# The ScalarE table that holds exponential and logarithm, loaded once in front of the differential attention of a two-block transformer kernel

## What is computed

```python
def diff_attention(q, k, v, lam, rel_bias):        # 4 heads of 2 x 64
    logits = einsum('bqhcd,bkhcd->bhcqk', qb, k) * scale + bias
    logits = where(mask, logits, -inf)
    p = softmax(logits)
    attn = p[:, :, 0] - lam * p[:, :, 1]
    return einsum('bhqk,bkhd->bqhd', attn, v)

def stick_breaking_attention(q, k, v):             # 8 heads of 64
    z = einsum('bqhd,bkhd->bhqk', qb, k) * scale
    log_1mb = where(mask, log_sigmoid(-z), 0.0)
    rem = cumsum(log_1mb, reverse=True) - log_1mb
    a = where(mask, exp(log_sigmoid(z) + rem), 0.0)
    return einsum('bhqk,bkhd->bqhd', a, v)
```

## Time and profile before

| | us |
|---|---|
| median of three runs | 2185.65 |
| lowest, highest of them | 2185.64, 2187.31 |
| the profiled execution, its own time | 2184.85 |
| its span in the trace (first to last instruction) | 2182.8 |

### The profile page before, as it was taken

One profiled execution on the slowest core, in us unless ns is written; L12 is line 12 of the kernel. 1 busy time (PEld: TensorE's weight loads), 2 busy tenths in 40 slices (PEclk: granted clock), 3 DMA queues, 4 the chain that ended last, 5 costly groups with the idle time before them and its releaser, 6 DMA issues.

```text
span 2182.8 us, 41798 instructions
## 1 busy us (share of the span) xinstructions
PE 2061.7 (94%) x17356; PEld 1271.0 (58%) x17356; DVE 863.7 (40%) x1472; ACT 477.2 (22%) x752; POOL 360.0 (16%) x389
## 2 busy tenths in 40 slices
PE   6999898599999999999999999979998998999998
PEld 5888766136434544443343333337775777888887
DVE  4454434433333323333332332333655443444444
ACT  4251433000000000000000000024445723122221
POOL 1010000112232222222232222231201200000000
PEclk9999998799999999999999999979998999999999
DMA  6333113899999999999999999963111021233231
GB/s 236 113 122 128 58 39 138 343 347 404 409 407 402 411 405 405 401 410 402 401 407 400 404 406 397 401 224 107 58 58 39 1 75 61 77 103 109 77 109 45
DMA packets 157311, 520.47 MB, mean 238 GB/s; under 512 B 16412, under 2 KB 71760, under 8 KB 124400
## 3 DMA queue, kind: packets, MB, share of 16 engines
q1 hardware_dynamic: 136480, 494.96, 57.9%
q0 software_dynamic: 20784, 24.85, 4.8%
HBM read 509.61 MB, written 18.88 MB: 242 GB/s over the span
## 4 chain that ended last, share of the span: by engine, by line
PE 63%; DMA 6%; SPq 5%; DVE 3%; ACT 2%; issue 1%; POOL 1%; ACTq 0%; DVEq 0%; POOLq 0%
PE ps L1973 24%; PE ps L1987 11%; PE ps L392 8%; PE ps L394 8%; PE ps L393 8%; DMA ring_a<-in_w_gate_up 4%; DMA ring_a<-in_w_down 2%; SPq L569 2%; SPq L567 2%; PE ps L1882 1%; POOL rstd L466 1%; PE ps L494 1%; PE ps L1874 1%; PE ps L1892 1%; PE ps L1835 0%
## 5 line engine op out<-in xcount | busy, mean ns | idle before, releaser
L1973 PE MATMUL ps<-ring_a,xe 128*32 128x512 f32 x3912 | 438.9, 598 | 12.0 <-DVE xe L1584 10.3
L1987 PE MATMUL ps<-ring_a,act_t 128*32 128x256 f32 x6000 | 335.2, 379 | 4.9 <-DMA ring_a<-in_w_down 3.0
L1973 PEld LDWEIGHTS ps<-ring_a,xe 128*32 128x32 f32 x3912 | 129.5, 111 | 294.1 <-issue 253.0
L1987 PEld LDWEIGHTS ps<-ring_a,act_t 128*32 128x32 f32 x6000 | 209.9, 110 | 137.4 <-issue 22.7
L1973 PE MATMUL ps<-ring_b,xe 128*32 128x512 f32 x2232 | 253.2, 594 | 0.0
L392 PE MATMUL ps<-xt_hi,hi 128*128 128x512 f32 x576 | 228.3, 396 | 5.6 <-DVE xt_lo L507 4.7
L394 PE MATMUL ps<-xt_hi,lo 128*128 128x512 f32 x576 | 226.3, 393 | 0.0
L393 PE MATMUL ps<-xt_lo,hi 128*128 128x512 f32 x576 | 225.8, 392 | 0.0
L1075 ACT ACTIVATE glu<-glu 128x768 f32<-128x768 f32 x32 | 27.0, 845 | 659.7 <-DVE glu L1591 618.4
L759 POOL DMA_INDIRECT x_rows<-ye,idx x96 | 154.3, 1608 | 37.8 <-issue 37.8
L1973 PEld LDWEIGHTS ps<-ring_b,xe 128*32 128x32 f32 x2232 | 76.9, 110 | 142.7 <-issue 132.6
(11 more groups left out here) (299 smaller groups left out, 2443.0 us busy)
## 6 DMA issues: line engine op xcount, KB each, us to landing
ring_a<-in_w_gate_up SPq DMA_DIRECT2D x163, 1024.0 KB
ring_a<-in_w_down SPq DMA_DIRECT2D x125, 1024.0 KB
ring_b<-in_w_gate_up SPq DMA_DIRECT2D x93, 1024.0 KB
raw<-in_w_in SPq DMA_DIRECT2D x20, 1024.0 KB, 7.7
raw<-in_w_gate SPq DMA_DIRECT2D x11, 1024.0 KB, 5.4
raw<-in_w_up SPq DMA_DIRECT2D x11, 1024.0 KB, 5.4
raw<-in_w_down SPq DMA_DIRECT2D x11, 1024.0 KB, 4.9
raw<-in_w_out SPq DMA_DIRECT2D x8, 1024.0 KB, 5.1
```

The costliest lines, as they stand in the source:

```text
L1973: last = pe.matmul(ps[QUAD * j:QUAD * j + QUAD, g, :], xe[:, g, QUAD * k:QUAD * k + QUAD], w[:, j, :, :, :], start=k == 0, stop=k == KT - 1)
L1987: last = pe.matmul(y_block(g, j), act_t[:, g, QUAD * (2 * c + h):QUAD * (2 * c + h) + QUAD], w[:, h, QF * j:QF * j + QF], start=c == 0 and ...
```

## The change

One line stands in `scalar_program` ahead of the first exponential of the differential attention. It loads the table that the compiler calls `natural_log_exp_and_others`, which holds both functions.

```diff
--- before.py
+++ after.py
@@ -980,6 +980,7 @@
                     i = copy(skT(2 * (c - B_SK) + n), bank)
                 i.then_inc(SB.evacuated[g % 4], 1)
 
+            act.preload_act_table_set("natural_log_exp_and_others")
             diff_exp(0)
             for n in range(DH * T):
                 diff_evac(n)
```

## The result

The changed kernel took 2172.53 us, the median of four runs from 2170.76 to 2174.62, beside 2186.22 for the kernel before in the same comparison. The ratio is 0.9941, with a 95% interval of 0.9926 to 0.9956: 13.7 us less where I had forecast 8.4. The time lies 1.0 us under the lower end of the range. The prediction was wrong in size, right in sign and, as the runs show, in its path.

The account below looks back on a forecast made before the run. A chain of waits with four table loads was taken to bound the kernel up to head 3's logits, then PE. 5.5 + 0.7 + 2.2 = 8.4 us off 2184.85, plus 0.80 for the median: 2177.3 us, range 2173.5 to 2181.5.

Parts of the forecast that it names:

- the second slow stretch: TensorE at 1.2 GHz in logits 3 and cumulation 2; costs 3.9 us, of which 2.2 was taken as gain.
- My own estimate of both at about 1682: Logits of head 3: without loads ready at about 1681.9, with PE free near 1682.0, within half a microsecond.
- slow stretches elsewhere: Slow clock stretches behind the stick-breaking stage: 1.7 us allowed either way, taken as 0.
- Loads on the chain: Four table loads ahead of the logits of head 3, worth 5.1 to 5.6 us together; 5.5 taken.
- Head 7: Two loads before head 7: removal shortens PE's 1.35 us wait at cumulation 7; 0.7 us taken.
- The ten hidden loads: Ten of the 16 removed loads, covered by waits for DVE or PE or by PE's work; credited with nothing.
- The added load: Load ahead of the differential attention's first exponential, inside ACT's 1.57 us idle time; cost 0, at most 1.3 us.
- The first slow stretch: TensorE at 1.2 GHz after its first wait, 1664.7 to 1671.4; worth nothing, as DVE's scaling sets head 2.
- Rival 1: TensorE falls to 1.2 GHz again near logits 3: only 6.2 us gained, median 2179.4; chance 0.31.
- Rival 2: The four chain loads were hidden by other waits: gain between none and 2 us, 2185.6 to 2183.6; chance 0.07.
- Rival 3: A table switch flushes ACT, so four chain loads give up to 10.4 us, not 5.5; 2173.2; chance 0.04.
- Rival 4: The joint table lengthens exponentials in both attentions: 2195.3 us at 0.4 us each; chance 0.03.

Follow-up runs that it names:

- e7: Changed kernel plus seven unread matmuls in TensorE's first wait, ahead of cumulation 0; 2176.81 us.
- e12: Changed kernel with two of the chain's four loads put back, before the logarithms of heads 0 and 1; 2179.40 us.
- e6: Kernel before, all 16 loads kept, with DVE's eight scaling instructions spread over heads 1 to 4; 2176.18 us.
- e5: Kernel before, all 16 loads kept, with seven unread matmuls in TensorE's wait ahead of the logits of head 3; 2180.56 us.
- e10: Changed kernel with two loads put back, before the logarithm of head 7 and the weights of head 6; 2176.68 us, a single run.
- e1: Changed kernel measured again with no edit; 2172.48 us.
- e3: Changed kernel with the ten loads put back whose removal was credited with nothing; 2175.62 us.
- e11: Changed kernel with the same ten covered loads put back, measured once more; 2172.68 us.
- e4: Changed kernel with its one load moved from the differential attention to the front of the stick-breaking attention; 2172.67 us.
- e2: Changed kernel with four loads put back, before the logarithms of heads 0, 1 and 2 and the weights of head 1; 2181.90 us.

## Why the prediction was wrong in size

**The step that failed is the clock's.** The prediction priced the second slow stretch at 3.9 us and then took 2.2, "a little over half". The trace has 3.88. The reason is not that the clock puts up with waits, as my nearest row had suggested: the wait before logits 3 vanished wholly, since PE's own work ended just as ACT was ready (e7 and e12 show that the clock would not have put up with 1.84 us). My own estimate of both at about 1682 said so, and I did not use it. That row, 1.35 us at head 7 with the clock unharmed, was one execution: e6 went unharmed too, but e5 and e10 fell at the very same wait.

**The second is the zero for slow stretches elsewhere**, with a base that was high. The profiled execution after had 2.53 us less ahead of the stage and 1.43 less behind it. Those come and go from run to run: in the differential attention a wait of 2.63 us, the same in all fourteen traces, was followed by a slow stretch in twelve, and not in the first of the changed kernel nor in e7. The stage begins at 1656.43 in e1, the same kernel as the changed one, and at 1654.43 and 1655.19 in e5 and e6, whose code is that of the kernel before up to there; from L494 to the end it takes 432.71 us in e1, and 431.68 and 431.30 in e5 and e6. Over 48 later runs before, and six of the changed kernel, the difference is 11.4 us and not 13.7. With 3.9 for the clock my sum would be 10.1. Of the 4.8 us by which the forecast of 2177.3 missed, the high base is thus 1.8 and the clock 1.7. What makes up the last 1.3 us I have not shown; it is within what single comparisons scatter (e3 and e11, one kernel, are 2.9 apart).

**The other terms held.** Loads on the chain: 5.5 taken, 5.64 measured, 1.41 for each of four, so that the overlap of two activations, 0.11 us, does belong to the price. Head 7: 0.72 taken from rows, 0.72 measured. The ten hidden loads: nothing in the stage of e3 and e11. The added load: nothing, with 0.27 us to spare as worked out. The first slow stretch: worth nothing in the first trace, as e7 shows, but where it reached into cumulation 1 (e1, e4, e10) the stage was 1.0 us longer, which the zero didn't foresee.

**The rivals.** Rival 1, the clock gives nothing back, is out: it did in both traces of the changed kernel. With 2.7 us more ladder (e12) it would have been right, and in e7 the clock fell again at a wait of 1.85 us. Rival 2, hidden anyway, is out by e2. Rival 3, a switch that costs about twice its row, gave the time nearest to what was first measured, 2173.2, by luck: a load put back moved the chain by 1.42 us (e2: 30.35 - 24.66 = 5.69 for four) and by 1.35 (e12: 2.69 for two). "ScalarE: Activation LUTs" in the Trainium skill adds a drain of about 1.38 us in its section on what ACT_TABLE_LOAD costs; these traces don't agree with it. Rival 4, slower exponentials, is out: 461 ns before and after in the stick-breaking attention, and 715 ns before and after for the exponentials of 512 columns in the differential one (L949).

## What to carry to other kernels

A short operation on ACT is worth its time only where the chain of waits passes through it, and there it can be worth nearly twice its time if the wait it lengthens leaves TensorE idle long enough to drop to 1.2 GHz (9.4 us for 5.1 us of loads in e2). So when a wait of PE is removed, count the slow groups behind it in full if PE's own work closes the gap, and nothing if a wait near 2 us or longer is left: in the stick-breaking attention each of the waits from 1.84 us up had a slow group behind it, and so had the 2.63 us of the differential one in twelve traces of fourteen. For a shorter wait give both outcomes and not the middle: behind the 1.34 to 1.35 us ahead of cumulation 7 it went either way. And where one ladder of waits has a load, a scaling and a sum in it, each of them is a handle: moving the scaling (e6, 7.7 us) was worth nearly as much as removing four loads (e2, 9.4 us).

## What the runs showed of the hardware

The same work, behind the same wait, is slowed in one execution and not in the next: the wait of 2.63 us in the differential attention left the clock at 2.4 GHz in the first trace of the changed kernel and not in the second, e1, and the 1.34 to 1.35 us wait ahead of cumulation 7 left the clock at 2.4 GHz in the kernel before and in e6, and was followed by a slow cumulation (6.14 and 6.09 us in place of 4.60) in e5 and e10. Cumulation 1 took 4.60 us in the first trace of the changed kernel behind a wait of 0.16 us, and 6.30 in the second behind one of 0.54. So one profile cannot price a clock term, and single runs of one kernel lie up to 8 us apart, 0.4%, though nothing in the program differs. In e5 matmuls without any use kept TensorE at 2.4 GHz and sped up the useful ones behind them by 3.9 us.
